# Up projection: every panel from the fifth by seven products, running sums seeded from PSUM bank to bank

## The reference

```python
def conv_ffn(xn, conv_prev, w_up, conv_w, conv_b, w_down):
    L = xn.shape[1]
    h = xn @ w_up                       # (576 x 1024) @ (1024 x 5632)
    hp = jnp.concatenate([conv_prev.astype(h.dtype), h], axis=1)
    hc = conv_b + sum(conv_w[j] * hp[:, j:j + L] for j in range(CONV_W))   # CONV_W = 3
    a, b = jnp.split(hc, 2, axis=-1)
    return (jax.nn.gelu(a) * b) @ w_down, hp[:, L:]
```

## Time and profile before

| | us |
|---|---|
| median of 3 runs | 1003.65 |
| lowest, highest | 1002.57, 1003.68 |
| the profiled execution, its own time | 1003.04 |
| span of its core | 1001.3 |

### The profile page before, as it was taken

How to read it: one execution, slowest core, us unless ns; L and a number is a source line. 1 busy time by engine, 2 the same in 40 slices (tenths; PEclk the granted TensorE clock), 3 DMA queues, 4 the chain that set the end, 5 groups by cost and what they waited for, 6 DMA issues and landing times.

```text
span 1001.3 us, 16975 instructions
## 1 busy us (share of the span) xinstructions
PE 969.6 (97%) x6682; PEld 923.6 (92%) x6682; DVE 597.8 (60%) x913; ACT 447.5 (45%) x720; POOL 134.2 (13%) x256
## 2 busy tenths in 40 slices
PE   5989999899999999999999999999999999999997
PEld 4989999899999999999997899999999999888886
DVE  5259998855423338814455678777777777632214
ACT  6355346677422245522124548455555445622112
POOL 3100000000022201002001154222222220000000
PEclk9989999999999999999999999999999999999999
DMA  6811222111242234447446452333333333312323
GB/s 185 181 61 43 85 62 66 43 44 44 66 141 66 67 101 143 141 150 254 131 131 227 134 166 84 85 85 85 84 84 84 84 84 105 109 63 85 115 85 115
DMA packets 104984, 104.31 MB, mean 104 GB/s; under 512 B 14018, under 2 KB 89138, under 8 KB 104928
## 3 DMA queue, kind: packets, MB, share of 16 engines
q1 hardware_dynamic: 98480, 80.54, 27.0%
q0 software_dynamic: 6448, 22.99, 6.6%
HBM read 89.84 MB, written 13.67 MB: 103 GB/s over the span
## 4 chain that ended last, share of the span: by engine, by line
PE 87%; DVE 6%; ACT 3%; issue 2%; DMA 1%; POOL 1%; SPq 0%; DVEq 0%; ACTq 0%
PE ps L1798 10%; PE ps L1800 10%; PE ps L1799 10%; PE ps L1807 7%; PE ps L1808 7%; PE ps L1809 7%; PE ps L2095 5%; PE ps L2097 5%; PE ps L2096 5%; PE ps L2119 3%; PE ps L2121 3%; PE ps L2120 3%; PE ps L1964 2%; PE ps L1817 1%; PE ps L1818 1%
## 5 line engine op out<-in xcount | busy, mean ns | idle before, releaser
L1798 PE MATMUL ps<-xs,whi 128*128 128x288 f32 x608 | 184.2, 303 | 0.0
L1800 PE MATMUL ps<-xs,wlo 128*128 128x288 f32 x608 | 179.9, 296 | 0.0
L1799 PE MATMUL ps<-xs,whi 128*128 128x288 f32 x608 | 179.8, 296 | 0.0
L1284 DVE TENSOR_TENSOR wlo<-raw,whi 128x2048 fp32r<-128x2048 f32 (+2 forms) x45 | 99.9, 2220 | 122.7 <-ACT whi L803 122.5
L803 ACT ACTIVATE whi<-raw 128x2048 fp32r<-128x2048 f32 (+2 forms) x47 | 86.1, 1832 | 96.1 <-PE ps L1809 77.9
L2095 PE MATMUL ps<-xs,whi 128*128 128x288 f32 x416 | 122.7, 295 | 1.5 <-DVE wlo L1614 0.9
L2097 PE MATMUL ps<-xs,wlo 128*128 128x288 f32 x416 | 122.6, 295 | 0.0
L2096 PE MATMUL ps<-xs,whi 128*128 128x288 f32 x416 | 122.5, 294 | 0.0
L1798 PEld LDWEIGHTS ps<-xs,whi 128*128 128x128 f32 x608 | 115.0, 189 | 0.7
L1799 PEld LDWEIGHTS ps<-xs,whi 128*128 128x128 f32 x608 | 115.0, 189 | 0.4
L1800 PEld LDWEIGHTS ps<-xs,wlo 128*128 128x128 f32 x608 | 114.7, 189 | 0.0
(11 more groups left out here) (344 smaller groups left out, 2195.3 us busy)
## 6 DMA issues: line engine op xcount, KB each, us to landing
raw<-in_w_in SPq DMA_DIRECT2D x21, 1024.0 KB, 5.8
raw<-in_w_up SPq DMA_DIRECT2D x22, 512.0 KB, 4.0
raw<-in_w_up SPq DMA_DIRECT2D x44, 256.0 KB, 4.4
raw<-in_w_down SPq DMA_DIRECT2D x10, 1024.0 KB, 5.1
raw<-in_w_out SPq DMA_DIRECT2D x6, 1024.0 KB, 5.0
gate_scratch<-stage POOLq DMA_DIRECT2D x16, 288.0 KB, 2.8
gates_in<-gate_scratch POOLq DMA_DIRECT2D x8, 576.0 KB, 4.2
raw<-in_w_branch_gla SPq DMA_DIRECT2D x4, 1024.0 KB, 5.0
```

Source lines behind the costliest of these rows:

```text
L1284: nc.vector.tensor_tensor(wlo[:, p % 2, 0:n], raw[:, p % 2, 0:n], whi[:, p % 2, 0:n].bitcast(F32), ALU.subtract).then_inc(lo_ready, 1)
L1798: pe.matmul(out, wh[:, k, c0:c0 + P], xh[:, k, t], start=(k == 0), stop=False)
L1799: pe.matmul(out, wh[:, k, c0:c0 + P], xl[:, k, t], start=False, stop=False)
L1800: ins = pe.matmul(out, wl[:, k, c0:c0 + P], xh[:, k, t], start=False, stop=(k == kn - 1))
```

## The change: what it does

1. **All panels from j = 4 by seven products** (18 in place of 9). PE's program is `seven_products` for each, in the order product 1, then *product 3 of the panel before*, 6, 2, 7, 5, 4. Product 3 (`third_product`) thus runs inside the next panel, in the same banks as its own panel; a last one follows the loop.
2. **Sums carried in PSUM.** ACT copies the bank of product 1 to the next bank (`seed_y`, L1276), on which products 6 and 4 accumulate, and that after product 6 to the next (`seed_z`, L1284), on which 5 and 3 accumulate. DVE's u_sum, v_sum and rows_12 are gone; ACT copies product 7's bank to `p7` (L1293), and DVE adds it in rows_22 (L1857) and rows_21 (L1863, L1864). rows_12 is a plain copy on ACT (L1308).
3. **Splits in pieces.** a1, a2, b2 are split one by one (ACT L1238, DVE `quad_lo` L1840, 128x512 each), the sums in two (ACT L1254, DVE `sums_lo` L1848, 128x1024 each).
4. **Odd panels' block sums in phase one.** SP loads the four blocks (L618 to 621) into one of four buffers that lie in places free there, DVE makes the four sums in place (slots 62, 63, 66, 67, 71, 81, 85, 92, 95), and SP stores 1 MB to `sums_scratch` in HBM. In the up projection SP loads that MB in place of the panel (L669), and a1, a2, b2 apart (L677, 683, 685) into `qraw`, which is the place of `qlo`, each when the product that reads its place is done.
5. **Both first taps of a panel** now stand behind its rows_12 and behind rows_22 and rows_21; ACT's order and DVE's in a pair are new (`own_panel`, `saved_panel`, `last_panel`). POOL's two stores of the attention state stand earlier, before the first load of `silu_in`.

The core of the diff:

```diff
+SEVEN0 = 4
+SEVENS = KF - SEVEN0
+SAVED = [j for j in range(SEVEN0, KF) if j % 2]
+SAVED_BUFFER = [0, 1, 0, 1, 0, 2, 3, 2, 3]
+SAVED_SLOT = [62, 63, 66, 67, 71, 81, 85, 92, 95]
 def seven(j):
-    return j >= 4 and j % 2 == 0
+    return j >= SEVEN0
...
+            def saved_load(k):          # SP
+                b, j = SAVED_BUFFER[k], SAVED[k]
...
+                d = saved[b][:, :].rearrange("p (k n) -> p k n", n=P)
+                sp.dma_start(d[:, 0:4, :], b_quads(j, 4)).then_inc(saved_in[b % 2], 16)
...
+            def saved_store(k):
+                b = SAVED_BUFFER[k]
+                sp.wait_ge(saved_summed, 4 * k + 4)
+                sp.dma_start(sums_dram[k], saved[b][:, :]).then_inc(saved_out[b % 2], 16)
...
+            with sp.Fori(2, KF // 2 - 1) as i:
+                q = quads(i)
+                own_sums(i + 1)
+                more_quads(*q)
+                saved_sums(i + 1)
...
+            def seed_y(i, r):           # ACT
+                b, s = 4 * (1 - r), order(i, r)
+                act.wait_ge(prod_done[1], s + 1)
...
+                nc.scalar.activation(ps[:, b + 1, 0:HALF], ps[:, b, 0:HALF], ACT.Copy).then_inc(y_seeded, 1)
+            def seed_z(i, r):
+                b, s = 4 * (1 - r), order(i, r)
+                act.wait_ge(prod_done[6], s + 1)
...
+                nc.scalar.activation(ps[:, b + 2, 0:HALF], ps[:, b + 1, 0:HALF], ACT.Copy).then_inc(z_seeded, 1)
...
+                elif op == "sums":      # DVE, phase one
+                    b = saved[SAVED_BUFFER[n]]
+                    s1, s3, s2, s4 = (b[:, 512 * i:512 * i + 512] for i in range(4))
+                    dve.wait_ge(saved_in[SAVED_BUFFER[n] % 2], 64 * saved_turn(n))
+                    nc.vector.tensor_tensor(s1, s3, s1, ALU.add).then_inc(saved_summed, 1)
...
-            def u_sum(i):
-            def v_sum(i):
-            def rows_12(i):
+            def own_panel(i, after_plain=False):   # DVE
+                quad_lo(i, 0, 2)
+                if not after_plain:
+                    rows_21(i - 1, 1)
+                conv(i - 1, 1, 0)
+                conv(i - 1, 1, 1)
+                quad_lo(i, 1, 0)
+                gated(i - 1, 1)
+                rows_22(i, 0)
+                sums_lo(i, 1, 1)
+                quad_lo(i, 1, 1)
+                sums_lo(i, 1, 0)
+            def saved_panel(i):
+                rows_21(i, 0)
+                conv(i, 0, 0)
+                block_sums(i + 1, 0)
+                quad_lo(i, 1, 2)
+                block_sums(i + 1, 1)
+                quad_lo(i + 1, 0, 0)
+                rows_22(i, 1)
+                conv(i, 0, 1)
+                sums_lo(i + 1, 0, 1)
+                quad_lo(i + 1, 0, 1)
+                gated(i, 0)
+                sums_lo(i + 1, 0, 0)
...
+            def seven_products(i, r, before=None):  # PE
+                s, x = order(i, r), 4 * (1 - r)
+                pe.wait_ge(a1_lo, s + 1)
...
+                product(1, x, qa1, b11, True)
...
+                    third_product(*preceding(i, r))
+                pe.wait_ge(s24_lo, s + 1)
+                pe.wait_ge(y_seeded, s + 1)
+                product(6, x + 1, quads(r, 2), t2, False)
+                pe.wait_ge(a2_lo, s + 1)
+                product(2, x, qa2, b21, False)
+                pe.wait_ge(s13_lo, s + 1)
...
+                product(7, x + 3, quads(r, 1), t3, True)
+                pe.wait_ge(z_seeded, s + 1)
+                product(5, x + 2, quads(r, 0), t1, False)
+                pe.wait_ge(b2_lo, s + 1)
+                product(4, x + 1, qb2, t4, False)
```

More of the change, by code:

```diff
@@ L250, in seven, with splits, saved_turn @@
 def seven(j):
[L251 removed]
+    return j >= SEVEN0
+def splits(p):
+    return p + 1 if p < DOWN0 else p + 1 - SEVENS
+def saved_turn(k):
+    return sum(b % 2 == SAVED_BUFFER[k] % 2 for b in SAVED_BUFFER[:k + 1])
 def plain_rows_done(i, r, g):
[L256 to L260 removed]
+    return 2 * (2 * i + r) + g + 1
 def preceding(i, r):
@@ L559, in _ @@
             load_x(1)
-            for p in range(UP0 + 2):
+            for p in range(UP0 + SEVEN0):
                 load(p)
+                for what, k in SAVED_MOVES.get(p, ()):
+                    if what == "in":
+                        saved_load(k)
+                    else:
+                        saved_store(k)
                 if p == 0:
@@ L572, in _, with own_sums @@
                     sp.dma_start(wgu_in[0:RANK, :], A["w_gla_gate_up"][0]).then_inc(wgu_loaded, 16)
[L573 to L579, removed]
+            def own_sums(i):
+                if isinstance(i, int) and i == 2:
+                    sp.wait_ge(lo_ready, UP0 + 3)
+                else:
+                    sp.wait_ge(a1_lo, order(i, -1))
+                    sp.wait_ge(a2_lo, order(i, -1))
+                    sp.wait_ge(b2_lo, order(i, -1))
+                for d, s in up_loads(2 * i, up_slot(0)):
+                    sp.dma_start(d, s).then_inc(raw_loaded[up_slot(0)], 16)
@@ L580, in _ @@
+            own_sums(2)
+            saved_sums(2)
+            with sp.Fori(2, KF // 2 - 1) as i:
[3 more added lines that the diff above has]
+                saved_sums(i + 1)
+            q = quads(KF // 2 - 1)
+            load(DOWN0)
+            more_quads(*q)
+            for p in range(DOWN0 + 1, NP):
                 load(p)
             sp.wait_ge(x1_saved, 16 * TILES)
-            sp.wait_ge(h_ready, plain_rows_done(KF // 2 - 1, 1, 1))
+            sp.wait_ge(prod_done[3], SEVENS)
@@ new lines, in quads, with third_product @@
+            def quads(r, k):
+                c = slice(512 * k, 512 * k + 512)
+                return whi[:, up_slot(r), c], wlo[:, up_slot(r), c]
+            def third_product(i, r):
+                pe.wait_ge(c22_ready, order(i, r) + 1)
+                product(3, 4 * (1 - r) + 2, quads(r, 3), b22, False)
+            def seven_products(i, r, before=None):
+                s, x = order(i, r), 4 * (1 - r)
+                pe.wait_ge(a1_lo, s + 1)
+                if before is None:
+                    pe.wait_ge(h_ready, plain_rows_done(1, r, 1))
+                else:
+                    pe.wait_ge(c11_ready, s - 1)
+                product(1, x, qa1, b11, True)
+                if isinstance(i, int) and s == 0:
@@ L2166, in _ @@
-            pe.wait_ge(c21_ready, KF // 2 - 2)
+                for r in range(2):
+                    seven_products(i, r, before=(i - 1, r))
+            third_product(KF // 2 - 1, 1)
             for q, job in enumerate(DOWN_JOBS):
```

447 lines of the change are left out of this document (275 added, 172 removed).

## The result

| | before | changed |
|---|---|---|
| median, us | 1003.66 | 992.0 |
| lowest to highest | 1002.57 to 1005.45 (4) | 991.49 to 993.72 (4) |
| ratio to before | | 0.9888 (0.9873 to 0.9903) |
| span of the profiled execution | 1001.3 | 990.3 |
| panel 4's first matmul to the down projection's first | 214.92 | 203.16 |

Forecast: 992.5, range 989.8 to 998.8. The last two lines come from the timelines of PE. They repeat: the second trace of the changed kernel (experiment 10) has 203.16 and 149.88, with a span 2.4 us longer.

What follows compares the result with a forecast made beforehand. PE's instruction count was taken as the bound: −14.04 matmuls, +0.9 seed, +1.9 chain, +0.1 end sum to −11.1 us, 991.9 from the profiled 1003.04; with the median 0.6 higher, 992.5 was named, range 989.8 to 998.8.

Steps and rivals of the forecast that it cites:

- Removed from PE: Up projection: nine odd panels go from 96 to 84 matmuls, saving 1.56 us each, −14.04 us.
- Seed: Panel 4's product 6 waits uncovered for ACT's bank-to-bank copy after product 1: +0.9 us, bounds 0.7 to 1.4.
- Chain: Odd panels' product 1 waits for a1's low part, 0.27 us late in seven pairs: +1.9 us, bounds 0 and 4.2.
- Even panels' chain: Steps to the next even panel's first product: 7.64 us against five products, 7.97; 0.33 to spare, no cost.
- DVE's load: DVE's work per pair in the up projection: 20.3 of 22.32 us (91%), plus about 1 us waiting per panel.
- Phase one: Odd panels' block sums fit into DVE's idle time: cost 0, bounds 0 and 5 us.
- a2's landing: a2's load, issued about 7.0 us into the even panel, must land by 12.8; hidden by 1.1 us at worst.
- the rival's price: Late a2 load (6%): each us beyond 5.8 stops PE once in each of 8 pairs; above 7.4, slower.
- End: Panel 21's product 3 comes last and waits for rows_22: +0.1 us, bounds 0 and 0.5.
- the chain did not hold fully: Rival (20%): steps to odd panels' product 1 counted 0.3 us too long; PE waits only at panel 4, 990.6 us.
- DVE is not the bound: Rival (19%): DVE's work plus two tap waits sets a period of 23.3 us per pair, 998.6 us.
- the late landing: Rival (6%): a2's load lands late behind 1 MB, PE waits at odd panels' product 2; 1009.8 us, slower.

Runs made afterwards that it cites:

- experiment 10: The changed kernel again, unedited, beside the kernel with three edits on the same chip: 993.87 us (991.48 to 994.54), ratio to before 0.9888.
- experiment 1: Changed kernel with a1's low part made between the two convolutions on DVE and its hi part one step earlier on ACT: 992.03 us, stretch 201.93.
- experiment 5: Changed kernel with one more ACT copy of product 6's bank, 0.3 us, ahead of the second seed: 994.31 us, stretch 205.43.
- experiment 6: Changed kernel with one more DVE addition of 128x512 at the end of each panel, 1.2 us per pair: 993.07 us, stretch 203.35.
- experiment 4: Kernel before with only the change's phase-one part added (block sums loaded, made, stored, never read; POOL's stores earlier): 1003.35 against 1003.36 us, ratio 1.0001.
- experiment 8: Changed kernel with an extra, unread copy of 1 MB issued by SP ahead of a2's load: 1006.75 us, ratio to before 1.0020.
- experiment 9: Changed kernel with the extra 1 MB copy ahead of a2's load, and ACT's first odd-panel seed ahead of a2's split: 1004.47 us, ratio 1.0011.

## Why the prediction was right, step by step

- *Removed from PE, −14.04.* Without the seed's and the chain's losses the stretch is 203.16 − 0.80 − 1.23 = 201.13, against 214.92: −13.79. A pair of 14 products takes 22.34 and not 22.32, which over nine pairs is 0.18 of the missing 0.25; the rest is rounding in the durations that I took from one pair.
- *Seed, +0.9.* Measured 0.80. ACT read the bank 0.32 after the start of its last matmul (638.77 to 639.09), not 0.49; the copy took 0.40 and not 0.39, and PE's restart 0.22 (639.49 to 639.84 − 0.13) and not 0.16. A copy from bank to bank takes about as long as one to SBUF, as the changed kernel's groups of ACT between 640 and 840 us show (busy, mean ns, then the idle time before):

```profile
L1293 ACT ACTIVATE p<-ps 128x288 f32<-128x288 f32 x18 | 7.2, 402 | 2.9 <-PE ps L2335 2.9
L1284 ACT ACTIVATE ps<-ps 128x288 f32<-128x288 f32 x18 | 7.1, 392 | 18.3 <-PE ps L2335 18.3
L1308 ACT ACTIVATE ha<-ps 128x288 f32<-128x288 f32 x17 | 7.0, 410 | 10.3 <-PE ps L2335 10.3
L1276 ACT ACTIVATE ps<-ps 128x288 f32<-128x288 f32 x17 | 6.8, 398 | 5.9 <-PE ps L2335 5.9
```

  By the Trainium skill ("Perfetto Trace Analysis", section "Optimizing Scalar/DVE Operations") the copies to `ps` should be about 0.04 shorter than those to `p` and `ha`, an estimate from its overheads for SBUF and PSUM; here they are about 0.01 shorter, and the measurement decides.
- *Chain, +1.9.* Right in place, sign and number of pairs; measured 7 × 0.175 = 1.23 (experiment 1), and its slope is one to one (experiment 5). Against my steps: 0.16 less at the bank's reading (708.58 to 708.91), 0.14 more between rows_12 and the tap (709.22 to 709.95 is 0.73, I had 0.59), PE's restart 0.24, I had 0.29. The two errors of about 0.15 nearly cancelled, which is luck: either of them alone, times seven, is 1.0 us, beside a term of 1.23. The list of waits shows 0.6 us from panel 4 on, where from start to start PE loses 0.80 + 1.23 = 2.03. My sign of being wrong (waits of under 1 or over 6 us) thus has to be read from start to start, and so read it was not met.
- *Even panels' chain, nothing.* Held: no gap at their first product.
- *DVE's load.* 44.74 of 50 is 89%, I had 91% (start to start). The waits for taps are 18.1 us over 17, 1.06 each, as I had (1.0). I had called DVE all but a second bound for that. The waits are slack: 1.2 us of work per pair went into them (experiment 6).
- *Phase one, 0.* Held alone (experiment 4) and in the whole.
- *a2's landing, hidden.* Held, with less to spare than I said. It landed 4.8 us after an issue 7.56 us into the even panel (711.49 − 703.93), where I had 4.7 at worst and 7.0: 12.36 in all, against the 12.8 at which it must have landed by my count. What I missed is who stands behind the wait: on ACT it is the next panel's seed, which ended at 717.58, and PE's product 6 began at 718.47; less a restart of 0.22 that leaves 0.7 us. In experiment 8 a2 landed 14.8 us into the even panel, 2.0 beyond my 12.8, and cost 1.7 us per pair without the lower clock: the rival's price (1 us for each us) nearly held, though by way of the seed. Its threshold did not. My 7.4 us from issue to landing were counted from an issue at 7.0; experiment 8 has the issue at about 8.0, and there 6.8 us were enough to be slower than before.
- *End, +0.1.* No wait showed for product 3 of the last panel. From the down projection's first matmul to the end 0.28 us more pass than before; 0.24 of them PE loses at the two transposes, which wait for POOL's last copies. I had not looked at that.
- *Sum.* −13.79 + 0.80 + 1.23 + 0.28 = −11.48; ahead of panel 4 the trace is 0.48 longer (636.82 to 637.30), of which 0.46 are there at 70 us already (the same matmul starts at 70.09 and at 70.55), before anything changed: −11.0, the difference of the spans. The forecast's −11.1 is nearer to this than its terms are to theirs, since one was too large by 0.7 and another too small by 0.25. That it stands 0.5 us from the median says little, as executions lie 3 us apart.

The rivals: the chain did not hold fully (990.6), DVE is not the bound, phase one holds nothing up, and the late landing did not happen. But it is only 2 us away, and with it the change was slower than before (experiment 8).

## What to carry to other kernels

Where a change takes work off the bounding engine and shortens its period, take each product that needs something fresh, and count the chain of hand-overs that makes it against the work that the engine has in the meantime. A difference of 0.2 us per period is a real loss that neither the busy share nor the list of waits shows, only the distance from start to start. Here one instruction moved forward on DVE and one on ACT took it away.

An engine at 90% with two idle microseconds per period is not the bound as long as work can move into its idle times; try it with a dummy instruction.

Of every wait on a DMA ask which instructions stand behind it on the waiting engine. Here PE first stopped at one of those, and not at the product that uses the data. To move that one forward was not enough: apart from the lower clock's 1.5 us it gave back 0.6 of 13.4, since the next ones behind the landing were late too (experiment 9).

## What the runs showed of the hardware

- PE's granted clock fell to 0.50 (1.2 of 2.4 GHz) behind some single waits. In experiment 8 PE stood still for 2.48 us from start to start (674.24 to 676.72) and then ran at the lower clock until 680.27 (windows as above; the clock is the third number from the end):

```profile
674.00:677.00 3.00, 0.81 (x7) 0.61 (x6) 1.05 (x2) 1.62 (x5) 0.00 (x0) 0.99 0.12 37
677.00:680.00 3.00, 3.00 (x14) 3.00 (x13) 2.88 (x6) 2.44 (x4) 1.51 (x4) 0.50 0.36 71
```

  These are 14 matmuls where 23 would stand; summed from start to start the lower clock cost 1.5 us. Stops of 1.10 to 1.98 us in that run's other pairs were followed by none.
- The same wait went either way from one trace to the next. Behind a wait of 1.48 us for ACT in phase one the kernel before (at 186.29) ran on with its matmuls 0.12 apart, and the changed one (at 186.78) with 0.21, until 190.13. Behind a wait for ACT near 217 the changed kernel ran on at a clock of 1.00 in its first trace (218 to 221, wait 1.90 us) and of 0.55 in experiment 10's (wait 1.85 us).
- What such a stretch costs depends on what follows. The one at 187 put the changed kernel 1.94 us behind the kernel before at 190.13, and at 195.43 only 0.64 were left, against 0.49 ahead of it: the kernel before had waited there 0.77 us for DVE, and the changed one did not. The one at 218 stayed: experiment 10's trace is 0.74 us behind the first one ahead of it and 2.24 behind it, and panel 4 begins at 639.66 and not 637.30. That is the difference of their spans.
- POOL's two copies of 128x2 ahead of the transposes took long while DVE was busy without a break from 841.06 to 847; the same pair takes 0.32 us at 709.86:

```profile
709.86 0.32 POOL L875 COPY convs<-ha 128x2 f32 x2 [3.30 <-ACT ha L1308]
...
841.20 5.12 POOL L875 COPY convs<-ha 128x2 f32<-128x2 f32 x2 [9.02 <-ACT ha L1308]
```

  PE's transposes then came 0.24 us late. The kernel before has such copies too (2.80 us at 703.42, while DVE is busy). Why they are slow was not tried.
